# Split weights moved to four offsets modulo 512 bytes, and every second chunk's products streamed backwards, in a two-block transformer kernel

## What is computed

```python
    def block(args):
        xb, ib, gb = args
        u = expert_down[ib]
        a = jnp.einsum('pd,ped->pe', xb, u).astype(jnp.float32)
        act = jax.nn.gelu(a, approximate=False) * gb
        v = expert_up[ib]
        return jnp.einsum('pe,ped->pd', act.astype(xb.dtype), v)
...
        x = x + jnp.square(jax.nn.relu(h @ w_up[l])) @ w_down[l]
```

## Time and profile before

| | us |
|---|---|
| median of 3 executions | 1323.48 |
| lowest, highest | 1318.81, 1326.25 |
| span of the profiled execution, first to last instruction | 1308.6 |
| around the span (the median less the span) | 14.9 |
| TensorE busy in the span | 1269.3 (97%) |
| VectorE busy | 986.7 (75%) |
| ScalarE busy | 729.2 (56%) |
| GpSimd busy | 301.5 (23%) |

### The profile page before, as it was taken

The page is one execution under the profiler, slowest core; times in us unless marked ns, Lnnn a source line. Parts: engine busy times, 40 slices in busy tenths (PEclk is TensorE's granted clock), DMA queues, the critical chain, the costliest instruction groups (busy, mean ns, idle before and its releaser), DMA issues.

```text
span 1308.6 us, 19970 instructions
## 1 busy us (share of the span) xinstructions
PE 1269.3 (97%) x7982; PEld 1133.7 (87%) x7982; DVE 986.7 (75%) x1712; ACT 729.2 (56%) x1131; POOL 301.5 (23%) x186
## 2 busy tenths in 40 slices
PE   5999979999999999999999999999989999999999
PEld 5878869999999999998888888888867687899987
DVE  5988998899999889985777777767666465755555
ACT  3565535555655699984544444444455455554543
POOL 0125010278876678350000000000000013000000
PEclk8999989999999999999999999999989997999999
DMA  9964679977778778889978787878554440555552
GB/s 369 368 242 148 217 257 361 315 209 222 242 255 265 218 236 245 292 283 359 326 271 302 272 305 272 304 274 302 212 197 149 165 155 27 192 193 193 193 192 97
DMA packets 138878, 317.11 MB, mean 242 GB/s; under 512 B 24991, under 2 KB 71456, under 8 KB 132898
## 3 DMA queue, kind: packets, MB, share of 16 engines
q1 hardware_dynamic: 101698, 265.42, 56.6%
q0 software_dynamic: 23072, 16.86, 7.0%
q10 hardware_dynamic: 14016, 33.56, 6.7%
HBM read 280.61 MB, written 35.20 MB: 241 GB/s over the span
## 4 chain that ended last, share of the span: by engine, by line
PE 88%; DVE 5%; DMA 4%; ACT 1%; issue 1%; SPq 1%; DVEq 0%; ACTq 0%
PE ps L647 11%; PE ps L646 11%; PE ps L648 11%; PE ps L658 11%; PE ps L660 11%; PE ps L659 11%; PE ps L624 3%; PE ps L625 3%; PE ps L626 3%; PE ps L943 1%; DMA wring<-in_w_in 1%; DVE w_lo L1699 1%; PE ps L995 1%; PE ps L818 1%; DMA peer_arena<-gates_of_second 1%; DMA arena<-in_ada_t 1%
## 5 line engine op out<-in xcount | busy, mean ns | idle before, releaser
L1699 DVE TENSOR_TENSOR w_lo<-wring,w_hi 128x1024 fp32r<-128x1024 f32 (+1 forms) x404 | 493.1, 1226 | 167.2 <-ACT w_hi L1227 163.0
L1227 ACT CAST w_hi<-wring 128x1024 fp32r<-128x1024 f32 (+1 forms) x404 | 419.5, 1046 | 237.0 <-PE ps L648 139.0
L646 PE MATMUL ps<-hT_hi,w_hi 128*128 128x256 f32 x1344 | 373.4, 278 | 1.4 <-DVE w_lo L1699 1.4
L648 PE MATMUL ps<-hT_hi,w_lo 128*128 128x256 f32 x1344 | 372.9, 277 | 0.0
L647 PE MATMUL ps<-hT_lo,w_hi 128*128 128x256 f32 x1344 | 372.9, 277 | 0.0
L1651 POOL DMA_INDIRECT gates_of_second<-late x128 | 244.2, 1908 | 139.3 <-issue 56.9
L646 PEld LDWEIGHTS ps<-hT_hi,w_hi 128*128 128x128 f32 x1344 | 253.9, 189 | 1.8 <-issue 1.5
L647 PEld LDWEIGHTS ps<-hT_lo,w_hi 128*128 128x128 f32 x1344 | 252.3, 188 | 0.3
L648 PEld LDWEIGHTS ps<-hT_hi,w_lo 128*128 128x128 f32 x1344 | 252.3, 188 | 0.0
L658 PE MATMUL ps<-w_hi,a_hi 128*128 128x512 f32 x624 | 245.3, 393 | 3.1 <-DVE w_lo L1699 3.1
L660 PE MATMUL ps<-w_hi,a_lo 128*128 128x512 f32 x624 | 244.8, 392 | 0.0
(11 more groups left out here) (326 smaller groups left out, 1504.4 us busy)
## 6 DMA issues: line engine op xcount, KB each, us to landing
wring<-in_peer_down SPq DMA_DIRECT2D x32, 2048.0 KB
wring<-in_peer_up SPq DMA_DIRECT2D x32, 2048.0 KB
wring<-in_w_in SPq DMA_DIRECT2D x11, 2048.0 KB
pages<-in_ada_t POOLq DMA_DIRECT2D x32, 512.0 KB, 5.8
acts_by_expert<-pages ACTq DMA_DIRECT2D x32, 512.0 KB
peer_arena<-acts_by_expert SPq DMA_DIRECT2D x32, 512.0 KB, 8.6
wring<-in_w_up SPq DMA_DIRECT2D x8, 2048.0 KB
wring<-in_w_down SPq DMA_DIRECT2D x8, 2048.0 KB
```

What stands on the lines that cost most here:

```text
L646: pe.matmul(o, hi[:, k, :], hT_hi[:, k, :], start=(k == 0), stop=False)
L648: mm = pe.matmul(o, lo[:, k, :], hT_hi[:, k, :], start=False, stop=(k == KC - 1))
L1227: act.copy(split_part(kind, w_hi, u, width(kind, j)), part_of(kind, wring[:, n % RING, :], u, width(kind, j))).then_inc(split_hi, 1)
L1699: dve.tensor_tensor(lo, part_of(kind, wring[:, n % RING, :], u, width(kind, j)), hi, ALU.subtract)\
```

## The change

The two edits:

1. **Places.** Each of the four parts in w_hi and in w_lo gets 16 floats (64 bytes) of room behind it. Part u therefore lies 64*u bytes further on, modulo 512. The gaps are set anew: wring and part 0 of both w tiles begin at 416, so that parts 0 to 3 begin at 416, 480, 32 and 96 (w_hi and w_lo alike). hT_hi and hT_lo stay at 32; a_hi, a_lo and onehot move to 480. The stationary slice less the moving one is then, for parts 0 to 3: in column_part -128, -64, 0 and +64 bytes; in row_part +64, 0, -64 and -128; in token_part +128, +64, 0 and -64. Two small tiles, kcn and kcq, are taken out of the tile zeros to make room.
2. **Direction.** In column_part and row_part of "wq", "dn", "ex" and "up" chunks with odd j, the moving operand is read from its last column to its first, and the output is written from its last column to its first. The "down" chunks, column_half and all token products stay forward.

On every engine the sequence of instructions, their shapes and their waits are as before; only addresses and steps differ. All line numbers from L52 on grow by one to five.

```diff
@@ -49,6 +49,7 @@
 SLOT = KC * CHUNK
 PARTS = 4
 PART = SLOT // PARTS
+SKEW = 16
 RING = 2
 EPS = 1e-6
 
@@ -248,11 +249,12 @@
         modc = sb("modc", [P, 6 * KC])
         gains = sb("gains", [P, 5, KC])
         small = sb("small", [P, 7, HD])
-        sb("gap_of_weights", [P, 120])
+        sb("gap_of_weights", [P, 72])
         wring = sb("wring", [P, RING, SLOT])
-        w_hi = sb("w_hi", [P, PARTS, PART], F32R)
-        w_lo = sb("w_lo", [P, PARTS, PART], F32R)
-        sb("gap_of_acts", [P, 16])
+        w_hi = sb("w_hi", [P, PARTS, PART + SKEW], F32R)[:, :, 0:PART]
+        sb("gap_of_rests", [P, 64])
+        w_lo = sb("w_lo", [P, PARTS, PART + SKEW], F32R)[:, :, 0:PART]
+        sb("gap_of_acts", [P, 176])
         adab = sb("adab", [P, 6 * KC])
         trig = sb("trig", [P, 2, NB, HD // 2])
         zeros = sb("zeros", [P, ZEROS])
@@ -267,8 +269,8 @@
         gatec = sb("gatec", [P, NB, NH, 3])
         mx = sb("mx", [P, 2, NB, R])
         sm = sb("sm", [P, 2, NB, R])
-        kcn = sb("kcn", [64, 2, HD])
-        kcq = sb("kcq", [64, HD])
+        kcn = zeros[0:64, 0:2 * HD].rearrange("p (u d) -> p u d", u=2)
+        kcq = zeros[0:64, 2 * HD:3 * HD]
         kcst = sb("kcst", [64, 4])
         kcmpT = sb("kcmpT", [P, 64])
         peT = sb("peT", [P, 2, NPAIR])
@@ -638,26 +640,26 @@
                 if half == 1:
                     mm.then_inc(parts_used, 1)
 
-            def column_part(bank, u):
+            def column_part(bank, u, turn=slice(None)):
 
                 hi, lo = (v[:, u, :].rearrange("p (k n) -> p k n", n=P) for v in (w_hi, w_lo))
-                o = psf[:, bank * 512 + u * T:bank * 512 + (u + 1) * T]
+                o = psf[:, bank * 512 + u * T:bank * 512 + (u + 1) * T][:, turn]
                 for k in range(KC):
-                    pe.matmul(o, hi[:, k, :], hT_hi[:, k, :], start=(k == 0), stop=False)
-                    pe.matmul(o, hi[:, k, :], hT_lo[:, k, :], start=False, stop=False)
-                    mm = pe.matmul(o, lo[:, k, :], hT_hi[:, k, :], start=False, stop=(k == KC - 1))
+                    pe.matmul(o, hi[:, k, :], hT_hi[:, k, turn], start=(k == 0), stop=False)
+                    pe.matmul(o, hi[:, k, :], hT_lo[:, k, turn], start=False, stop=False)
+                    mm = pe.matmul(o, lo[:, k, :], hT_hi[:, k, turn], start=False, stop=(k == KC - 1))
                 mm.then_inc(parts_used, 1)
 
-            def row_part(u, first, last):
+            def row_part(u, first, last, turn=slice(None)):
 
                 hi, lo = (v[:, u, :].rearrange("p (s n) -> p s n", n=512) for v in (w_hi, w_lo))
                 for b in range(NB):
                     t = slice(b * P, (b + 1) * P)
                     for half in range(2):
-                        o = ps[:, 4 + 2 * b + half, :]
-                        pe.matmul(o, a_hi[:, u, t], hi[:, half, :], start=first, stop=False, skip_group_check=True)
-                        pe.matmul(o, a_hi[:, u, t], lo[:, half, :], start=False, stop=False, skip_group_check=True)
-                        mm = pe.matmul(o, a_lo[:, u, t], hi[:, half, :], start=False, stop=last, skip_group_check=True)
+                        o = ps[:, 4 + 2 * b + half, turn]
+                        pe.matmul(o, a_hi[:, u, t], hi[:, half, turn], start=first, stop=False, skip_group_check=True)
+                        pe.matmul(o, a_hi[:, u, t], lo[:, half, turn], start=False, stop=False, skip_group_check=True)
+                        mm = pe.matmul(o, a_lo[:, u, t], hi[:, half, turn], start=False, stop=last, skip_group_check=True)
                 mm.then_inc(parts_used, 1)
 
             def out_part(j, u):
@@ -728,13 +730,16 @@
                         mm = pe.matmul(o, hT_lo[:, k, t], hi[:, kk, :], start=False, stop=(k % 4 == 3))
                 mm.then_inc(parts_used, 1)
 
+            def direction(j):
+                return slice(None, None, -1 if j % 2 else None)
+
             def by_columns(kind, j):
 
                 n = NTH[kind, j]
                 bank = free_banks(n)
                 for u in range(PARTS):
                     split_landed(n, u)
-                    column_part(bank, u)
+                    column_part(bank, u, direction(j))
 
             def turn_round(src, what):
 
@@ -959,7 +964,7 @@
                 for u in range(PARTS):
                     pe.wait_ge(S["a_lo_ready"], j * PARTS + u + 1)
                     split_landed(NTH["ex", j], u)
-                    row_part(u, j == 0 and u == 0, j == STEPS - 1 and u == PARTS - 1)
+                    row_part(u, j == 0 and u == 0, j == STEPS - 1 and u == PARTS - 1, direction(j))
 
 
             pe.wait_ge(emptied_by["act"], emptied_count("dn", STEPS - 1))
```

## The result

| | median us | lowest to highest | executions |
|---|---|---|---|
| before, in this comparison | 1322.78 | 1318.66 to 1329.11 | 8 |
| changed | 1333.24 | 1329.95 to 1336.28 | 8 |

The ratio is 1.0114, with a 95% interval of 1.0080 to 1.0148: the change makes the kernel slower by about 1%. The forecast was no change; 1333 lies inside the stated range, on the side of the second rival.

What follows compares the result with a forecast made beforehand. PE, busy 97% of the span, was taken to bound the kernel by matmul count times pitch. Terms +0.6 + 1.0 - 2.6 = -1.0 us on 1308.6 plus 14.9 around it gave 1322.5 us; forecast's own range 1317 to 1329, whole range 1294 to 1347.

Steps and rivals of the forecast that it cites:

- the second rival: Column and row products: the new mixture of distances holds the longer pitch; +24 us, 1347 us; chance of slower distances 0.22.
- PE's own two operands as the cause: All matmuls: 6.6, 11 and 15 ns of each pitch lost to PE's two reads or how they lock.
- Distance -128 has no row here ... I take the nearest, no difference: Column and row parts at distances without profile rows: priced like the nearest known distance, no difference.
- I take 0 for the pitch itself: Backward chunks, 2112 column and 768 row products: the negative step itself changes the pitch by 0.
- 0.6 + 1.0 us: Places: distance 0 costs 2 ns more on 282 column products (0.6 us) and a quarter of 1920 row products (1.0).
- the price at 0: Row products at distance 0: 2 ns more on a quarter of 1920, 1.0 us.
- The bound that I worked out for the columns: Worst case for places: all column products at the 118 ns pitch, (4224 - 1128) x 4.5 = +13.9 us.
- the upper bound: Direction's worst case: backward columns and rows fall to plain fp32 pace, +380 us; the places' worst is +13.9 and +8.1.
- Half of the long-pitch stretch given back: Column products at 118 ns: direction changes at chunk boundaries disturb the lock and recover half the loss, -2.6 us.
- worse distances: Columns from 240 to 450 us go from 113 to the longer pitch, rows rise too; +24 us, 1347 us; chance 0.22.
- Fewer collisions: All products: opposite directions and new distances ease the meeting of PE's two reads; -26 us, 1298 us; chance 0.33.
- A backward stream is slow: Every second chunk: one element per fetch instead of a burst; up to +380 us, a tenth +38, 1361 us; chance 0.08.

Runs made afterwards that it cites:

- direction_only: Kernel before with only the second edit: odd chunks backwards, addresses as before; median 1323.11 us, ratio 1.0072.
- rows_256: Kernel before with gap_of_acts at 96 floats, so the distance in row products is 256 bytes instead of -64; median 1309.60 us, ratio 0.9951.
- mended: Kernel before, row distance 256; first three products backwards in column parts that open a chunk or follow one-hot products; 1306.68 us, ratio 0.9903.
- rows_0: Kernel before with gap_of_acts at 32 floats, so the distance in row products is 0 instead of -64; median 1310.90 us, ratio 0.9962.
- onehot_64: Kernel before with the one-hot products' stationary slice 448 bytes lower, so their distance is +64 instead of 0; median 1313.27 us, ratio 0.9982.
- before_again: Kernel before, no edit, profiled once more; median 1323.11 us, profiled span 1327.1 us.

## Why the prediction was wrong

**What bounds the kernel, and PE's own two operands as the cause**: right. The loss is in the pitch, PE's waits and the other engines' work are unchanged, and moving one operand against the other by 64 bytes changes the pitch by up to 6.6 ns in columns and 7 in rows, forward. That it is their reads which meet stays an inference.

**"Distance -128 has no row here ... I take the nearest, no difference"**: the step that failed, with "I take 0 for the pitch itself" for the direction. In place of 0.6 + 1.0 us, the places alone gave a ratio of 1.0095, 12 us at the medians. Three of the four parts lost the distance +64, at which alone the short order had been seen, and took 119.2, 117.5 and 120.4 ns. The nearest rows were not near: a single product at distance 0 between others at +64 shows no loss (0.12 us) where a whole part takes 120.4 ns each. For rows the price at 0 had the wrong sign in a uniform kernel, -2.2 ns and not +2; in the changed kernel it was near (230 against 228.5), and the unpriced +64 and -128 were the dear ones, at 233.3. The bound that I worked out for the columns, that all are at the long pitch (+13.9 us), came nearly true: 118.0 in the first window.

**Direction**: a backward column stream takes 117.8 ns where a forward one takes 113.4, and a backward row 4 to 5 ns more than a forward one. In direction_only that is a ratio of 1.0072. Both losses lie far below the upper bound. (Its term for rows is worked out wrongly: twice 216 ns less 228.5 is 203.5, not 212, which makes the bound +373 us and not +380.) "Half of the long-pitch stretch given back" did occur as a mechanism, in forward chunks; its size was off, for each healed chunk came after a backward one at 117.8.

**The reference point**: the sum was set on one execution of 1310 us and the result on a median of 1323. I read the 4.5 ns between stretches as a property of the stretch; it was one of the execution. Had the spread of the three executions, 7.4 us, been held against the 1100 products at the long pitch, worth 5 us, the two would have been seen to be of one size. The stated range held 1333 all the same, by its width.

**Rivals**: "worse distances" came true, at its place (240 to 450 us from 113 to 118) and near its price: 24 us over the profiled span, measured 21 (from the median, its 1347 us was 14 too high). Its mechanism was half right: what makes the long pitch is the distance of three parts in four, and the backward stream in every second chunk. The disturbance at each part mostly heals: in the forward chunks of the windows shown the part at +64 is at 113.8. "Fewer collisions" is refuted for these addresses, but rows_256 and mended show that the loss it spoke of can be reduced. "A backward stream is slow" fell: +4.4 ns in 113. The rule for PSUM beside it (Trainium skill, PSUM — Partial Sum Buffer, Specifications: a pattern that isn't contiguous slows matmuls significantly) doesn't reach step -1 here. The other rule cited, two independent read ports in TensorE, so that nothing waits (Trainium skill, SBUF — State Buffer, Who interferes with whom), would give 0 for the places; by these runs the measurement decides against it: moving a_hi, a_lo and the tiles beside them by 64 bytes (rows_0) takes the rows from 228.5 to 226.2 ns, and moving the weights takes the columns from 113 to 120.

Open: what in the hardware has the period of 256 bytes, and what selects the order at +64 when a run of column products begins. The runs show that it differs between executions, that it lasts for hundreds of products, and that a stretch backwards can mend it. One-hot products do turn it, from short to long at +64 and +192 and from long to short at -192. Whether that is by their distance 0 or as a mere break is not settled, for onehot_64 began in the long order.

## What to carry to other kernels

Where PE never waits, divide a window's length by its count of matmuls and hold it against one column per tick: a few per cent above it can be a matter of where stationary and moving slices lie to each other (here 113 to 120 ns over 106.7; no distance came below 113). That costs only a little room to change, and is found by a sweep of 32 or 64 bytes over one period. Sweep each kind of product by itself and uniformly, since a single product at another distance showed nothing of what a whole part took.

Profile an execution more than once before a stretch's pitch is taken as its own. If executions of one kernel differ by more than the effect sought, look first at what differs between them; here that was worth 0.5 to 1%.

## What the runs showed of the hardware that I had not expected

- fp32r products of 256 columns at 2.4 GHz take 113.4, 117.5 to 118, 119 or 120 ns, those of 512 columns 226.5, 229 or 232 to 233, by the distance of the two slices modulo 256 bytes (in columns distance and place aren't told apart). The pitch doesn't follow VectorE's load: VectorE was busy 99% of the window at 113.0 ns, 96% of that at 117.5 (before_again) and 34% of that at 118.
- At some distances (+64, +192 and -192 in columns, -64 in rows) there are two pitches for the same code, 113.4 or 117.8, and 229 or 233. One holds for 10 to 400 us, and one execution can keep another than the next. Four products from another tile can turn it, either way.
- A stream with step -1, in SBUF and in PSUM, costs 4% in columns at +64 against the short order, none against the long one (117.8 both), and nothing or less in columns at distance 0 (118.3 against 120.4).
